# Mean squares of the norms moved into the stages in front of them, modulation chunks spread over other stages, routers loaded once: a two-block network on one core

## The reference, cut to what matters

```python
def rms_norm(x, g):
    xf = x.astype(jnp.float32)
    y = xf * lax.rsqrt(jnp.mean(xf * xf, axis=-1, keepdims=True) + EPS)
    return (y * g.astype(jnp.float32)).astype(x.dtype)
...
    groups = [tr(o).reshape(B, S, GROUP_WIDTH) for o in (oa, ob, oc, od)]
    mixed = jnp.concatenate([rms_norm(gr, group_out_g[i]) for i, gr in enumerate(groups)], axis=-1)
    x = x + mixed @ w_o
    u = jax.nn.relu(rms_norm(x, mlp_norm_g) @ w_up)
    return x + (u * u) @ w_down
```

## Time and profile before

| | before |
|---|---|
| median of 3 runs | 2951.38 us (2943.82 to 2954.22) |
| profiled execution | 2950.33 us |
| its span | 2948.5 us |
| PE / PEld busy | 2690.1 (91%) / 1697.2 (58%) |
| DVE / ACT / POOL busy | 1184.3 (40%) / 748.0 (25%) / 16.3 (1%) |
| mean granted clock of TensorE | 0.953 of full speed |
| HBM read, written | 543.19 MB, 2.10 MB |

### The profile page before, as it was taken

One profiled execution on the slowest core, in us unless ns is written; L12 is line 12 of the kernel. 1 busy time (PEld: TensorE's weight loads), 2 busy tenths in 40 slices (PEclk: granted clock), 3 DMA queues, 4 the chain that ended last, 5 costly groups with the idle time before them and its releaser, 6 DMA issues. The chain is left out here.

```text
span 2948.5 us, 37258 instructions
## 1 busy us (share of the span) xinstructions
PE 2690.1 (91%) x15640; PEld 1697.2 (58%) x15640; DVE 1184.3 (40%) x2230; ACT 748.0 (25%) x1518; POOL 16.3 (1%) x34
## 2 busy tenths in 40 slices
PE   8988999999899999888799999999889969988887
PEld 6745688787787878665633433433667755322223
DVE  5456433333566666665501111112546552111113
ACT  4344233332431222112211111111417621110101
POOL 0000000000000000000000000000010000000000
PEclk9989899999999999988899999999889989999998
DMA  4330323223310101013099999998240054999995
GB/s 184 136 143 1 143 86 114 86 86 138 116 43 17 59 15 59 1 57 116 1 347 362 352 353 342 352 343 317 89 173 2 6 196 198 430 430 430 429 430 246
DMA packets 52846, 547.69 MB, mean 186 GB/s; under 512 B 8231, under 2 KB 16295, under 8 KB 19656
## 3 DMA queue, kind: packets, MB, share of 16 engines
q1 hardware_dynamic: 52680, 545.31, 47.3%
HBM read 543.19 MB, written 2.10 MB: 185 GB/s over the span
## 5 line engine op out<-in xcount | busy, mean ns | idle before, releaser
L3055 DVE SCALAR_TENSOR_TENSOR residual<-experts_psc,mod,residual 128x512 f32<-128x512 f32 (+1 forms) x101 | 71.9, 716 | 434.1 <-PE experts_psc L2927 363.0
L2848 PE MATMUL experts_pg_l<-ring,moe_xe_l 128*64 128x512 f32 x728 | 192.5, 606 | 16.1 <-DMA ring<-in_moe_gu 11.7
L2848 PE MATMUL experts_pu_l<-ring,moe_xe_l 128*64 128x512 f32 x728 | 188.3, 595 | 0.0
L2869 PE MATMUL experts_py_l<-ring,experts_turn_l 128*64 128x512 f32 x752 | 172.2, 600 | 10.9 <-DMA ring<-in_moe_down 9.6
L3040 DVE TENSOR_TENSOR experts_y_low<-experts_py_l,experts_y_whole 64x512 fp32r<-64x512 f32 x64 | 44.1, 689 | 194.1 <-ACT experts_y_whole L2991 165.6
L2869 PEld LDWEIGHTS experts_py_l<-ring,experts_turn_l 128*64 128x64 f32 x752 | 52.0, 138 | 116.8 <-issue 99.3
L2974 ACT ACTIVATE experts_act_l<-experts_pg_l 128x512 f32<-128x512 f32 x32 | 19.1, 598 | 393.8 <-PE experts_pu_l L2848 393.8
L3029 DVE SCALAR_TENSOR_TENSOR experts_hid_l<-experts_act_l,moe_gate_rows,experts_pu_l 128x512 f32<-128x512 f32 x32 | 23.9, 747 | 229.9 <-ACT experts_act_l L2974 229.9
L2848 PEld LDWEIGHTS experts_pu_l<-ring,moe_xe_l 128*64 128x64 f32 x728 | 53.1, 138 | 104.0 <-issue 104.0
L685 PE MATMUL down_acc<-down_u_hi,down_w_hi 128*128 128x512 f32 x256 | 100.9, 394 | 5.5 <-DVE down_w_lo L712 5.5
L2848 PEld LDWEIGHTS experts_pg_l<-ring,moe_xe_l 128*64 128x64 f32 x728 | 45.5, 136 | 102.8 <-issue 82.2
(11 more groups left out here) (598 smaller groups left out, 5603.1 us busy)
## 6 DMA issues: line engine op xcount, KB each, us to landing
ring<-in_moe_gu SPq DMA_DIRECT2D x91, 2048.0 KB, 9.2
ring<-in_moe_down SPq DMA_DIRECT2D x47, 2048.0 KB, 9.1
ring<-in_ada_w SPq DMA_DIRECT2D x24, 2048.0 KB, 7.9
moe_wide_early<-in_moe_gu SPq DMA_DIRECT2D x9, 2048.0 KB, 30.3
normed<-in_moe_gu SPq DMA_DIRECT2D x9, 2048.0 KB, 30.3
moe_wide_high<-in_moe_gu SPq DMA_DIRECT2D x9, 2048.0 KB, 30.3
moe_wide_low<-in_moe_gu SPq DMA_DIRECT2D x9, 2048.0 KB, 30.3
ring<-in_w_up SPq DMA_DIRECT2D x8, 2048.0 KB, 7.8
```

Of the source, the lines that this page charges most:

```text
L2848: last = nc.tensor.matmul((pg_l, pu_l)[m][64 * half:64 * half + 64, :], xe_l[:, e, k, :], columns(n, 2 * kk + m, FH * half, FH), start=(k ...
L2869: last = nc.tensor.matmul(py_l[64 * half:64 * half + 64, :], turn_l[:, c, i, :], columns(n, c, FH * half, FH), start=(f == 0), stop=(f == ...
L3055: nc.vector.scalar_tensor_tensor(out=x[:, d, c0:c0 + n], in0=banks[bank][:, 0:n], scalar=gate[j][:, d:d + 1], in1=x[:, d, c0:c0 + n], op0= ...
```

## The change

1. A new class `MeanSquares` takes the place of `NormPart`. Squares, sums, mean, reciprocal and root of the six large norms are done at the end of the stage in front; the root's columns lie in `core.norm_col` over the stage's end. `norm_stage` keeps spread, gain, scale, shift and what modulation chunks it has, all of them behind the spread.
   - w_o, w_out, down and the experts: ScalarE squares each tile behind its add; TensorE sums by rows, a matmul of 32 equal columns of ones by 512 (or 256) tokens in one of four column groups (`row`); ScalarE copies the bank (`keep_rows`); 4 or 6 one-column matmuls finish the sum and turn it (`columns`). In down the context's squares are inside the loop.
   - hyena: ScalarE squares each tile of 768, VectorE adds six of the pairs between the outputs' adds, and TensorE has two sets of six one-column matmuls (`sums`).
2. Modulation chunks: MLA 5 to 3, group norm 0 to 3 (one ahead of its sums, two behind its spreads), norm_m 3 to 2, norm_h 4 to 3, norm_e 4 to 2, routing of layer 0 0 to 3, norm_s 2 to 0, axial 4 to 6, norm_f 2 to 0, routing of layer 1 0 to 2. In the routings a part uses one bank for its products and half of another for its turns, and stands on TensorE between the turned tokens and the places; the tenth half-tile of tokens is turned behind the first gathers.
3. Both layers' routers come in setup, in pieces of 1 KB, into one tile, with the slot numbers; the router matmul has the 32 columns of both layers, and the fold picks the layer's. The two loads and the memset at the start of each routing go.
4. `scatter_plan`: in layer 0 two scatters more behind two chunks near the end each (20 to 16 behind the last chunk), in layer 1 two behind each chunk of the last expert (10 to 8); the ones left over are put in another order.

The diff, cut:

```diff
-MOD_MLA, MOD_NORM_M, MOD_NORM_H, MOD_NORM_E, MOD_NORM_S, MOD_AXIAL, MOD_NORM_F = 5, 3, 4, 4, 2, 4, 2
+MOD_MLA, MOD_GROUPS, MOD_NORM_M, MOD_NORM_H, MOD_NORM_E, MOD_AXIAL = 3, 3, 2, 3, 2, 6
+MOD_ROUTE = (3, 2)
...
+    def square(self, act, k, c0=0, n=None):
+        n = self.tiles * P if n is None else n
+        self.core.nc.scalar.activation(self.core.h[:, k, c0:c0 + n], self.core.x[:, k, c0:c0 + n], ACT.Square).then_inc(self.squared.handle, 1)
...
+    def row(self, pe, bank, k, c0, n):
+        q = self.ROWS * (k % 4)
+        ins = self.core.nc.tensor.matmul(bank[q:q + self.ROWS, 0:n], self.core.ones[:].to_broadcast([P, self.ROWS]), self.core.h[:, k, c0:c0 + n],
+                                         start=(k < 4), stop=(k >= 4), tile_position=(0, q))
+        if k == KD - 1:
+            ins.then_inc(self.rowed.handle, 1)
+
+    def keep_rows(self, act, *parts):
+        for i, (bank, c0, n) in enumerate(parts):
+            act.wait_ge(self.rowed.handle, self.rowed.at(i + 1))
+            self.core.nc.scalar.copy(self.core.h[:, 0, c0:c0 + n], bank[:, 0:n]).then_inc(self.rows_kept.handle, 1)
+
+    def columns(self, pe, bank):
+        pe.wait_ge(self.rows_kept.handle, self.rows_kept.at(self.parts))
+        for t in range(self.tiles):
+            ins = self.core.nc.tensor.matmul(bank[:, t:t + 1], self.core.h[:, 0, t * P:(t + 1) * P], self.core.ones[:], start=True, stop=True)
+        ins.then_inc(self.summed.handle, 1)
...
@@ norm_stage
             @block.tensor
             def _(pe):
-                for i in range(early):
-                    part.step(pe, i)
-                norm.sums_pe(pe)
-                norm.spread_pe(pe)
-                for i in range(early, mod_chunks):
+                for i, (c0, n, g, sc, sh) in enumerate(streams):
+                    for t in range(n // P):
+                        at = c0 // P + t
+                        last = nc.tensor.matmul(spread_to[i][:, t * P:(t + 1) * P], core.norm_col[:, 2, at:at + 1].to_broadcast([P, P]), core.ident[:],
+                                                start=True, stop=True)
+                    last.then_inc(spread.handle, 1)
+                for i in range(mod_chunks):
                     part.step(pe, i)
...
@@ product_stage, PE, ACT, DVE
+                if ms:
+                    for j in range(KD):
+                        ms.await_squared(pe, j + 1)
+                        ms.row(pe, acc[0], j, 0, SEQ)
+                    ms.columns(pe, acc[0])
...
+                        if ms and c and k >= 4:
+                            await_kept(act, k - 4)
+                            ms.square(act, k - 4)
...
+                if ms:
+                    ms.invert(dve, acc[0])
...
@@ group_norm_stage, PE
+                part.step(pe, 0)
                 for g in range(G):
...
+                for i in range(1, MOD_GROUPS):
+                    part.step(pe, i)
...
@@ hyena_stage, PE
+                pe.wait_ge(sp_free.handle, sp_free.at(4 + spec_at(TURNS - 1, SP - 1)))
+                ms.await_paired(pe, KD - 2)
+                ms.sums(pe, spec[0], 0, True, False)
+                ms.await_squared(pe, KD)
+                ms.sums(pe, spec[0], KD - 1, False, True)
...
@@ route_stage
-                sp.dma_start(router[:, :, 0:E], ins["moe_router_2"][layer].rearrange("(k p) e -> p k e", p=P)).then_inc(loaded.handle, 16)
-                sp.dma_start(number[:], core.consts["slot_number"]).then_inc(loaded.handle, 16)
-                if not ctx:
+                if ctx:
+                    core.stream(sp, core.used)
+                else:
                     wide.load(sp, NS)
                     sp.wait_ge(tok_turned.handle, tok_turned.at(len(halves)))
                     wide.load(sp, NS + 1)
                     wide.load(sp, WideRing.ONCE)
+                    core.stream(sp, core.used)
                     sp.wait_ge(gathered.handle, gathered.at(nl))
...
-                    turn_half(10)
+                for i in range(part.n):
+                    part.step(pe, i)
                 pe.wait_ge(placed.handle, placed.at(1))
...
@@ scatter_plan
-        for _ in range(2 if (what, i) in SCATTER_TWO else 0) if ctx else range(1):
+        if ctx:
+            several = 2 if (what, i) in SCATTER_TWO or (i == 3 and e >= N_EXP - 2) else 0
+        else:
+            several = 2 if e == N_EXP - 1 else 1
+        for _ in range(several):
...
@@ experts_stage, PE
+                for i, (_, s, d) in enumerate(final):
+                    ms.await_squared(pe, i + 1)
+                    ms.row(pe, py_l if s == "l" else py_c, d, *span[s])
+                ms.columns(pe, py_l)
```

More of the change, by code:

```diff
@@ L347, in __init__ @@
         self.rooted = st.counter("norm_rooted", 1)
[L348 to L356 removed]
+        self.scale = 1.0 if pairs else D / self.ROWS
@@ new lines, in columns, with sums @@
+    def columns(self, pe, bank):
[3 more added lines that the diff above has]
+        ins.then_inc(self.summed.handle, 1)
+    def sums(self, pe, bank, k, first, last):
+        for t in range(self.tiles):
+            ins = self.core.nc.tensor.matmul(bank[:, t:t + 1], self.core.h[:, k, t * P:(t + 1) * P], self.core.ones[:],
+                                             start=(first and t == 0), stop=(last and t == self.tiles - 1))
+        if last:
+            ins.then_inc(self.summed.handle, 1)
@@ L414, in norm_stage @@
+def norm_stage(core, name, streams, mod=None, mod_chunks=0, out=None):
     nc = core.nc
-    h = core.h
+    x, h = core.x, core.h
     with Stage(core, name) as st:
-        norm = NormPart(core, st, streams, fresh)
+        spread_to = [st.ps(f"spread{i}") for i in range(len(streams))]
+        gain = st.sb("gain", [P, len(streams), KD])
+        gained = st.counter("norm_gained", len(streams))
+        spread = st.counter("norm_spread", len(streams))
         scaled = st.counter("norm_scaled", KD * len(streams))
@@ L433, in _ @@
             def _(act):
-                norm.squares(act)
-                for i in range(early):
-                    part.keep_row(act, i)
-                norm.root(act)
-                late = list(range(early, mod_chunks))
+                late = list(range(mod_chunks))
                 for i, (c0, n, g, sc, sh) in enumerate(streams):
@@ L468, with product_stage @@
 BUFS = 3
-def product_stage(core, name, widths, tokens, tiles, move, by, take, then=None):
+def product_stage(core, name, widths, tokens, tiles, move, by, take, then=None, squares=False):
     nc = core.nc
@@ L2133, in _ @@
                             centre(it + 1, i)
+                for j in range(KD):
+                    act.wait_ge(ip_dve.handle, added_at(TURNS - 1, "out", j))
+                    ms.square(act, j)
+                ms.root(act)
             @block.vector
@@ L2530, in _ @@
                 if ctx:
-                    for i in (8, 9, 10):
-                        high(i)
+                    high(8)
+                    high(9)
+                for i in range(part.n):
+                    part.keep_row(act, i)
                 for i in range(0, ng, 2):
@@ L2761, in scatter_plan @@
                 ready += [(2, ("c", e // 4, d)) for d in range(KD)]
-    for _, item in ready:
-        plan.append((last, *item, bank(spare + more)))
+    left = [item for _, item in ready]
+    rows = [item for item in left if item[0] == "l"]
+    context = [item for item in left if item[0] == "c"]
+    lag = len(rows) - len(context) // 2
+    for i in range(len(rows) + len(context) // 2):
+        for item in rows[i:i + 1] + (context[i - lag:i - lag + 1] if i >= lag else []):
+            plan.append((last, *item, bank(spare + more)))
     return plan
@@ L3018, in _ @@
                 keep_y(E - 1)
+                for m, s, d in final:
+                    act.wait_ge(added.handle, added.at(m + 1))
+                    ms.square(act, d, *span[s])
+                ms.keep_rows(act, *[(py_l if s == "l" else py_c, *span[s]) for s in streams])
+                ms.root(act)
             @block.vector
```

262 lines of the change are left out of this document (139 added, 123 removed).

## The result

| | before | changed |
|---|---|---|
| median of the runs shown with the prediction's result | 2950.72 us (n = 4) | 2915.09 us (n = 4) |
| again, in a later set | 2949.58 us (n = 9) | 2912.86 us (n = 4) |
| profiled execution | 2950.33 us | 2918.54 us |
| its span | 2948.5 us | 2916.7 us |
| PE, DVE, ACT busy | 2690.1, 1184.3, 748.0 | 2662.1, 1152.2, 770.5 |

The ratio of the changed kernel to the one before is 0.9879 (95% interval 0.9856 to 0.9902), and 0.9878 (0.9865 to 0.9892) the second time: 36 us faster, where 40 were forecast. One execution of the changed kernel, and one of the kernel before in a later set, took far longer (5417 and 8381 us, with a granted clock of 1.00); no reading rests on them, but the median of 2915.09 us counts the first, and without it it is 2911.64.

What follows compares the result with a forecast made beforehand. Layer 0's experts were taken as bound by TensorE and layer 1's by transfers, leaving the seams to gain; the terms summed to -40.2 us, from 2950.33 to 2910.1, forecast as 2911, own range 2903 to 2918, wider range 2897 to 2933.

Steps and rivals of the forecast that it cites:

- rival 2: TensorE at its lower clock in the tails, so last rows and columns cost more: 13 us, 2924; chance 15%.
- rival 4: The table load for the squares' root is not hidden in norm_f, norm_l and norm_s: 3.1 us, 2914; chance 5%.
- rival 6: Slower: added matmuls cost layer 0's expert loop granted clock; 2961 if it falls below 0.92; chance 4%.
- rival 5: Layer 1's gain is not passed on, its stream starting two loads short: +9.8 us, 2921; chance 4%.
- Rival 3: Moved chunks set the end in MLA, group norm, axial and routing 0: 11.5 us, 2922; chance 8%.
- W_out with norm_f: Seam behind w_out: 4.1 us saved from last add to spread, 2.3 by a stage end without chunks; -6.4.
- the routers' step: Routers' loads and slot numbers moved from the routings to the start: taken as 0 (-0.5 to 0.3).
- w_o with norm_m: Seam behind w_o: 4.1 us saved up to the spread, 0.8 by one turn less behind it; -4.9.
- Hyena and norm_e: Seam behind hyena, 14.37 us from last add to spread, would shrink to 5.9 (5.0 to 7.4); -8.5.
- Group norm: Going from 0 to 3 chunks, two behind the spread, makes w_o start later: +6.5 (5 to 8).
- MLA: With 3 chunks for 5, transposes start when k is turned, not queued behind chunks: -5.0 (-3.5 to -5.4).
- The tails of the experts: Scatters moved ahead leave fewer VectorE adds in both layers' tails; layer 0's full loop pays +1.8 (0 to 3.2).

Runs made afterwards that it cites:

- The run with waiting rows: The late version with TensorE waiting for all eight squares before the first row in w_out and w_o: 2907.73 us, ratio to the kernel before 0.9856.
- late version: The changed kernel with the loads of routers and slot numbers moved from setup to the start of the pairs stage: 2898.20 us, and 2897.22 once more.

## Why the prediction was right, and where it was wrong

**Right.** The direction, the size within 4 us, and the mechanism of all six seams: with one square, one row, one copy and the columns left behind the last add, the gaps came out within 0.3 us of the working in five of six. Where rows don't wait, norm_m's, norm_f's and norm_l's gap is 4.45 us in all profiles, so rows and columns did not take twice their prices (rival 2's cost, out). The root's table load is hidden by what the working named (rival 4 out, and with it the longer wait that the prediction names beside it). TensorE's clock stayed at 1.00 in the long loop (rival 6 out), and layer 1's stream was as fast as before, 428 GB/s for 430 (rival 5 out). Rival 3 is out as well: MLA's first eviction of the transposed heads follows VectorE's last operation without idle time, and routing 0 and the axial stage grew by 0.5 and 1.0 us. W_out with norm_f came out at -6.4 in both profiles of the changed kernel, but other profiles with the same code have up to -9.0, so that it is exact is luck.

**The total is luck in part.** It lies in the forecast's own range, 2903 to 2918, because 14.8 us that nobody had priced stand against gains that were larger than forecast, hyena's and norm_e's above all. With the routers loaded late the same change is 52 us faster (2897.22 for 2949.58), and the forecast of 40 would have been 12 short.

**Wrong, the routers' step.** The step reads "I take 0 (-0.5 to 0.3, an issue or two on SP)". It measured +14.8 in both profiles and 15.6 over the runs. I had priced the two loads where they left, at routings, where the router's issue took 0.38 us in the kernel before, and not where they arrived: behind the residual and the weights, where setup's barrier stands behind SyncE. None of the rivals had it. The profile of the kernel before showed no such wait. Its timeline of setup had a hint, two issues of the same residual's parts, 0.43 us at first and 0.83 for the last, but no row of it foretells 12 us: the last one, behind 8 MB, took 0.66.

```profile
5.09 0.83 SPq L230 DMA_DIRECT2D residual<-in_x_rows  x1
...
7.82 0.66 SPq L233 DMA_DIRECT2D residual<-in_ctx_rows  x1
```

**Wrong in sign, the clock.** Rival 2 had the lower clock as a cost of the change, and the terms of the sum left the clock out. The runs show a gain: the mean granted clock was 0.950 to 0.955 in the compared executions of the kernel before (those beside the experiments) and 0.963 to 0.968 in the changed kernel's. From 0.953 to 0.963 of the span is, by the two levels, 2 x 0.047 x 2948.5 = 277 us at the lower one before and 2 x 0.037 x 2916.7 = 216 after. The squares beside the adds keep TensorE at work through a seam: it is idle for 0.45 us ahead of w_o's last rows, where 2.99 stood ahead of norm_m's first chunk. The Trainium skill's page "TensorE: Matmul & The Clock Gate" (Part 1), by which activity lifts the throttle, had been read for the wrong side: the change adds activity where there was none. What this is worth in one seam depends on the execution. In the first profile norm_m's spread took 1.13 in place of 2.07 and w_o with norm_m came out 3.1 us beyond the forecast; in the second the spread took 1.75 and the term was -5.0, as forecast. Of the nine profiles with two chunks in norm_m and rows that don't wait, four have it at 7.2 us and a clock of 1.00, and five at 8.8 to 10.2 and 0.69 to 0.81. The same holds of up, down and norm_h (-11.1 and -8.6 for -8.9). The run with waiting rows doesn't settle it, since its norm_m is as long as in four of these five.

**Hyena and norm_e**, -15.0 for -8.5. The seam itself, from last add to spread, gave 9.6 (14.37 to 4.80; I had 8.5), as the sums ran at the upper level (2.81 us for all, row at 1363.85). Six more came inside hyena, from its first instruction to its last add, with the same 2632 matmuls (windows of before, then of the changed kernel):

```profile
749.58:1371.15 621.57, 573.15 (x2632) 451.36 (x2632) 389.84 (x664) 133.91 (x265) 0.55 (x10) 0.96 0.11 39
```

```profile
747.30:1362.84 615.54, 565.67 (x2632) 448.47 (x2632) 393.61 (x670) 139.46 (x272) 0.55 (x10) 0.97 0.12 43
```

The kernel before with nothing but the early loads took 617.4 there, so up to 4 us of the 6 lie within what its own executions differ by (granted clock 0.956 and 0.964; 0.969 in the changed kernel), which the change did not aim at. What sets that course of the clock stays open: it wasn't tried.

**Group norm** cost 4.1 and not 6.5 (the lower bound of my range was 5). From the start of the spreads to w_o's first instruction it took 13.7 us where I had 14.8, with both chunks' products at the upper level (1.92 each), and the spreads began 7.5 us into the stage and not 8.9, since behind chunk 0 the sums ran faster. In the late version's first profile these are 13.9 and 8.5, and the stage costs 5.3. **MLA** gave 3.6 in the first profile and 5.3 in the second, where 5.0 was forecast; the stage's granted clock is 0.72 in the first and 0.79 in the second (0.82 before). Over the study's profiles the two chunks are worth about 6 (averages of 47.8 and 41.7).

**The tails of the experts.** For fewer adds I had -2.1 in layer 0 and -1.2 in layer 1, and +1.8 for the scatters in layer 0's loop. In layer 1 the step holds: the changed plan is about 1.7 us shorter there. In layer 0 it fails: -0.3 forecast, +1.3 measured. Either the loop pays more than 1.8 or VectorE's adds aren't what ends that tail; no run here tells the two apart.

**The split of the sum.** Adding the terms one by one came near for the whole change and was wrong for its parts: without new places for the chunks, the mean squares bring 20.6 us and not the 39 that the list leaves them. The seams' savings hold only if the early chunks find another place.

## What to carry to other kernels

Price a transfer that is moved at the queue it moves into: a 128 KB load behind some megabytes in one queue held its issuer for 12 us, and a barrier passes that on to every engine. Work that fills an idle TensorE between two dense stretches can pay twice, by its own overlap and, in some executions, by the clock of what follows. One profile is not enough to price a stage of some microseconds by: take a second one of the same kernel first. Parts of a change that share cover (here squares and chunks in one stage) can't be priced apart; undo one to see what the other is worth.

## What the runs showed of the hardware

SyncE's issue of one load of 128 KB took 0.33 us in a stage with no large load in the queue, 0.42 near the start of setup, and 12.38 and 12.18 behind the large ones; the small load behind it took 2.52, and the 1 MB load ahead of it 0.68. Identical instructions differed by 5.5 us of 90 with the granted clock (1.00 against 0.91), from one execution to the next. A table load of 1.28 us on ScalarE was followed by the root 0.25 us after its end, on the root's own wait for VectorE; no further time of the switch shows.
